# Retention rounds with three unread 512-column products each, normalisations on ScalarE, and output tiles begun before the last mixed rows, in a two-layer attention block on Trainium2

## The chip, the core and the metric

The kernel runs on one core of one Trainium2 chip and uses the core's engines together: TensorE (PE in the profile; PEld is its loading of weights), VectorE (DVE), ScalarE (ACT), GpSimd (POOL), and SyncE (SP), which issues the DMAs. The metric is the time in microseconds of one launch, which covers both layers. An engine runs its instructions in the order in which they are written; between engines the order is made by semaphores alone.

## The reference

Two layers, each of a token mixer and a feed-forward part, on 1024 tokens of width 1024, in float32. The mixer has three kinds of heads whose results stand side by side: differential attention (512 columns), MLA (256) and retention (256). What the change touches is retention, the third:

```python
rel = pos[:, None] - pos[None, :]
decay = where(rel >= 0, exp(max(rel, 0) * log_gamma[h]), 0)
xi   = exp((pos + 1) * log_gamma)       # per head
zeta = exp((c - 1 - pos) * log_gamma)
inner = einsum('bnihd,bnjhd->bnhij', q, k) * decay
inner = einsum('bnhij,bnjhe->bnihe', inner, v)
new_state = einsum('bjhd,bjhe->bhde', k * zeta, v) + exp(c * log_gamma) * state
cross = einsum('bnihd,nbhde->bnihe', q, prev_states) * xi
o = inner + cross                       # (o - mean) * rsqrt(var + 1e-6), per head of 64
return silu(g) * (o * gn_w + gn_b)
```

There are 4 heads of 64 columns, in chunks of c = 128 tokens. The mixed rows then go through an output projection, `x = x + mixed @ w_out` (1024 by 1024), and through the feed-forward part.

## The kernel before

Every product of the reference is done as three products of TensorE on operands that are split in a high and a low part (hi·hi, hi·lo, lo·hi, the helper `split` with `products`, L718). ScalarE makes a high part by a copy that rounds, and VectorE or GpSimd the low part by subtracting it. An operand that has to stand with its columns on the partitions is transposed by TensorE into a PSUM bank (`take_ring` hands out the banks in turn and waits until an old one has been read), and the two evictions of the bank, ScalarE's high part and VectorE's low part, free it.

A layer runs through these stages, on each engine in the same order: norm and transposes of x, differential attention, MLA, retention, transposes of the mixed rows, output projection, feed-forward part. The projections for retention (q, k, v and gate of a unit in one row `r_z[n]` of 512 columns) are made during the MLA steps, by `ret_project`, in the bank Z_BANK (4), and VectorE turns q and k there by their rotary angles (`ret_rotate`).

**The retention rounds** are the stage that the change rewrites. A unit is one pair of heads in one chunk of 128 tokens: 16 units, 8 chunks of each of 2 pairs. TensorE's loop (L1034 to L1040) does in one round the transposes of one unit, the inner and state products of the unit before it and the output products of the one before that:

- `ret_transpose` (L978): three transposes 128x128, of q, k and of q times xi. ScalarE has made q times xi and k times zeta in `r_xzt` by four scalings of 64 columns per unit (`ret_scaled`). ScalarE and VectorE evict the three as `rt_hi` and `rt_lo` (128x384, L1820).
- `ret_inner` (L991): k·q for the two heads, three products each; then, except in the last chunk of a pair, the state product of k times zeta (`rk_hi`, `rk_lo`) with v (`rv`, high and low part side by side). VectorE multiplies the inner result by the decay table (`r_at`, L1830), and multiplies the state by its chunk decay and adds the product (`r_st`, L1840). ScalarE makes the high parts of both and GpSimd the low ones.
- `ret_output` (L1010): per head two products with `r_at` and, but for a pair's first chunk, two with the state (L1027, L1028).
- VectorE sums the two halves (`r_sum`, L1849), takes the moments (L1853, L1858), and once GpSimd has made the inverse root it normalises each of the two heads (`r_norm`, L1867). GpSimd multiplies by gn_w, adds gn_b and multiplies by the gate into `mixed_rows` (`ret_finish`).

The same rounds carry the split of the first half of w_out: four parts, ScalarE's high (L1158) and GpSimd's low (L2147), in rounds 0 to 3. SP loads decay, gn_w and gn_b (counted together by one semaphore, `ret_in`) when the last attention output has been read, since they lie where attention's buffers were, and the first use of any of them, `r_at` of unit 0, waits for all three.

**After the rounds** TensorE transposes all 8 tiles of `mixed_rows`: 64 transposes in 16 blocks of four (`transpose_rows`, L749), each block evicted to `ht_hi` by ScalarE (L1170) and to `ht_lo` by VectorE (L1607), over a ring of four banks. They start when all units are finished for the first half of the tiles. Then come 16 output tiles of 128 tokens by 512 columns, q = 0 to 15 in bank q % 4, each of 24 products 128x512 (8 blocks k of rows, three products each). VectorE adds a tile to X; from q = 4 on TensorE waits for the addition of tile q - 4. X comes back from DRAM in two halves (`x_back0`, `x_back1`), as its place holds other things in between; SP asks for the first when the transposes of the first four tiles are through, and for the second when all are.

Of the kernel before, what the change touches and what calls it, by code (L numbers as in the profile page):

```python
# [8 lines left out]
F32 = mybir.dt.float32  # L9
F32R = mybir.dt.float32r  # L10
# [92 lines left out]
def mla_back_rings():  # L103
# [25 lines left out]
    r_vlo=2 * T, r_take=2 * T, r_xz=2 * T, r_kzhi=2 * T, r_kzlo=2 * T, ri_done=2 * T, r_at=2 * T, r_athi=2 * T, r_atlo=2 * T,  # L129
    ro_done=2 * T, rs_done=2 * (T - 1), r_st=2 * (T - 1), r_sthi=2 * (T - 1), r_stlo=2 * (T - 1),  # L130
    r_bn=2 * T, r_mv=2 * T, r_ms=2 * T, r_rstd=2 * T, r_on=2 * T, r_gw=2 * T, r_gb=2 * T, r_mx=2 * T,
# [43 lines left out]
def constants():  # L175
# [6 lines left out]
    xi = np.exp((pos[:, None] + 1.0) * log_gamma[None, :])  # L182
    zeta = np.exp((P - 1.0 - pos)[:, None] * log_gamma[None, :]) * RET_DIM ** -0.5
    for p in range(RET_PAIRS):
        c[:, C_XZ + 4 * p:C_XZ + 4 * p + 2] = xi[:, 2 * p:2 * p + 2]
        c[:, C_XZ + 4 * p + 2:C_XZ + 4 * p + 4] = zeta[:, 2 * p:2 * p + 2]
        c[:64, C_CD + p] = np.exp(P * log_gamma[2 * p])
        c[64:, C_CD + p] = np.exp(P * log_gamma[2 * p + 1])
# [7 lines left out]
    rel = pos[None, :] - pos[:, None]  # L196
    decay = np.where(rel[:, None, :] >= 0, np.exp(np.maximum(rel, 0.0)[:, None, :] * log_gamma[None, :, None]), 0.0)
    return c, (decay * RET_DIM ** -0.5).astype(np.float32).reshape(P, RET_HEADS * P)


def hybrid_block_kernel(nc, x, positions, attn_norm, w_in, diff_lam_q1, diff_lam_k1, diff_lam_q2, diff_lam_k2,
                        diff_subln, mla_q_norm, mla_w_uq, mla_kv_norm, mla_w_ukv, ret_gn_w, ret_gn_b, w_out,
                        ffn_norm, w_gate, w_up, w_down, final_norm, out):
    const_np, decay_np = constants()
    const_dram = nc.inline_tensor(const_np, name="const_table").ap()
    decay_dram = nc.inline_tensor(decay_np, name="decay_table").ap()
# [79 lines left out]
    decay = sb("decay", [P, RET_PAIRS, 2 * P], F32, EREG)  # L286
    gn_w = sb("gn_w", [P, RET_W], F32, EREG + 2 * KB)
    gn_b = sb("gn_b", [P, RET_W], F32, EREG + 3 * KB)
    rt_hi = [sb(f"rt_hi{i}", [P, 3, P], F32R, HT + 12 * KB + 1536 * i) for i in range(3)]
    rt_lo = [sb(f"rt_lo{i}", [P, 3, P], F32R, HT + 17 * KB + 1536 * i) for i in range(3)]  # L290
# [3 lines left out]
    rv = [sb(f"rv{i}", [P, 2, 2, RET_DIM], F32R, HT + (22 + i) * KB) for i in range(5)]  # L294
# [8 lines left out]
    r_xzt = [sb(f"r_xzt{i}", [P, 4, 64], F32, HT + (35 + i) * KB) for i in range(3)]  # L303
    r_at = sb("r_at", [P, 2 * P], F32, HT + 38 * KB)
    r_at_hi = [sb(f"r_at_hi{i}", [P, 2 * P], F32R, HT + (8 + i) * KB) for i in range(2)]
    r_at_lo = [sb(f"r_at_lo{i}", [P, 2 * P], F32R, HT + (10 + i) * KB) for i in range(2)]
    r_st = sb("r_st", [P, P], F32, MREG + 13 * KB)
    r_sum = [sb(f"r_sum{i}", [P, 2, RET_DIM], F32, MREG + 13 * KB + 512 + 512 * i) for i in range(2)]
# [2075 lines left out]
```

## Time and profile before

| | us |
|---|---|
| median of 3 runs | 2777.3 |
| the runs | 2774.96, 2777.3, 2779.53 |
| the profiled execution: its time | 2776.76 |
| its span in the trace | 2775.0 |
| TensorE busy | 2597.4 (94%) |
| VectorE busy | 1560.8 (56%) |
| ScalarE busy | 1107.1 (40%) |
| GpSimd busy | 1039.7 (37%) |

The busy shares are means over the whole span. TensorE counts as busy for as long as a product or transpose of it is under way, at either of its clocks; the clock that it was granted stands in a row of its own of the page, and in a column of the table by stage (1.00 is 2.4 GHz, 0.50 is 1.2 GHz). In a timeline the time of a product reaches into the next one's, so the distance of two starts tells what one costs. The first layer's retention rounds lie at 561 to 636 us and the second's at 1933 to 2007.

### The profile page before, as it was taken

How to read it: one execution, taken by the hardware profiler on the slowest of the kernel's cores; microseconds unless marked ns; L12 is line 12 of the kernel's file. 1: busy time of each engine (PE TensorE's matmuls, PEld its weight loads, DVE VectorE, ACT ScalarE, POOL GpSimd, SP SyncE). 2: the span in 40 equal slices, each digit the busy share in tenths (PEclk: the TensorE clock that was granted, in tenths of full speed). 3: DMA queues.
4: the chain of work that ended last, by engine and by line, in shares of the span. 5: the costliest groups of instructions: out<-in, count | busy, mean ns of one | idle time of the engine just before them, and what ended most of it. 6: DMA issues, size and time to landing. Idle time of an engine off the chain costs nothing. (4 is left out here: it accounts for less than half of the span.)

```text
span 2775.0 us, 43012 instructions
## 1 busy us (share of the span) xinstructions
PE 2597.4 (94%) x12940; PEld 2228.0 (80%) x12940; DVE 1560.8 (56%) x3033; ACT 1107.1 (40%) x2567; POOL 1039.7 (37%) x1229
## 2 busy tenths in 40 slices
PE   6999988889999999999989998988998999999997
PEld 5999877767778888888879998776776888888886
DVE  4666554473455445477656765544726544545785
ACT  4444543352532232244444455434515232322444
POOL 3455522183154544301034554222812555442012
PEclk9999999958999999999999999998599999999999
DMA  5111101121223332483331101012022323335633
GB/s 173 28 36 41 30 15 37 38 84 61 103 73 110 106 110 93 148 292 96 103 107 31 34 19 39 6 37 89 32 91 76 111 84 104 110 104 207 231 95 122
DMA packets 238651, 243.06 MB, mean 88 GB/s; under 512 B 27904, under 2 KB 170752, under 8 KB 238464
## 3 DMA queue, kind: packets, MB, share of 16 engines
q1 hardware_dynamic: 238464, 240.83, 27.0%
q8 instruction: 86, 1.41, 0.2%
q14 instruction: 101, 0.83, 0.1%
HBM read 173.14 MB, written 67.63 MB: 87 GB/s over the span
## 5 line engine op out<-in xcount | busy, mean ns | idle before, releaser
L2319 POOL TENSOR_TENSOR fw_a_lo<-fw_a_raw,fw_a_hi 128x512 fp32r<-128x512 f32 x132 | 178.7, 1354 | 520.6 <-DVE fw_s_raw L1913 520.6
L2319 POOL TENSOR_TENSOR fw_s_lo<-fw_s_raw,fw_s_hi 128x512 fp32r<-128x512 f32 x176 | 231.4, 1327 | 54.6 <-ACT fw_s_hi L1422 54.6
L718 PE MATMUL banks<-ht_hi,da_hi 128*128 128x512 f32 x496 | 192.9, 389 | 0.0
L718 PE MATMUL banks<-ht_lo,da_hi 128*128 128x512 f32 x496 | 192.9, 389 | 0.0
L718 PE MATMUL banks<-ht_hi,da_lo 128*128 128x512 f32 x496 | 192.9, 389 | 0.0
L718 PE MATMUL banks<-w_diff_hi,ht_hi 128*128 128x384 f32 x512 | 181.2, 354 | 6.3 <-DVE ht_lo L1609 4.3
L718 PE MATMUL banks<-w_diff_hi,ht_lo 128*128 128x384 f32 x512 | 172.9, 338 | 0.0
L718 PE MATMUL banks<-w_diff_lo,ht_hi 128*128 128x384 f32 x512 | 172.8, 337 | 0.0
L2158 POOL TENSOR_TENSOR qk_rot<-rope_a,rope_b 128x512 f32<-128x512 f32 x64 | 82.6, 1291 | 211.7 <-DVE rope_b L1638 211.7
L1666 DVE TENSOR_REDUCE stats<-banks 128x1 f32<-128x1024 f32 (+3 forms) x192 | 138.3, 747 | 29.8 <-PE banks L919 24.9
L718 PE MATMUL banks<-h_t_hi,fw_s_hi 128*128 128x512 f32 x352 | 139.9, 398 | 12.2 <-DVE h_t_lo L1917 8.2
L718 PE MATMUL banks<-h_t_lo,fw_s_hi 128*128 128x512 f32 x352 | 139.0, 395 | 0.0
L718 PE MATMUL banks<-h_t_hi,fw_s_lo 128*128 128x512 f32 x352 | 138.9, 395 | 0.0
L1496 ACT ACTIVATE u_two<-u_two 128x512 f32<-128x512 f32 x42 | 26.6, 633 | 281.1 <-DVE u_two L2024 281.1
L718 PE MATMUL banks<-ht_hi,fw_a_hi 128*128 128x512 f32 x352 | 137.4, 390 | 0.9 <-POOL fw_a_lo L2319 0.9
L718 PE MATMUL banks<-ht_hi,fw_s_hi 128*128 128x512 f32 x352 | 137.0, 389 | 0.0
L718 PE MATMUL banks<-ht_hi,fw_a_lo 128*128 128x512 f32 x352 | 137.0, 389 | 0.0
L718 PE MATMUL banks<-ht_lo,fw_s_hi 128*128 128x512 f32 x352 | 137.0, 389 | 0.0
L718 PE MATMUL banks<-ht_lo,fw_a_hi 128*128 128x512 f32 x352 | 137.0, 389 | 0.0
L718 PE MATMUL banks<-ht_hi,fw_s_lo 128*128 128x512 f32 x352 | 137.0, 389 | 0.0
L1981 DVE TENSOR_TENSOR da_lo<-da_raw,da_hi 128x512 fp32r<-128x512 f32 x154 | 117.1, 760 | 22.6 <-ACT da_hi L1473 22.6
L1233 ACT ACTIVATE pt_hi<-banks 128x512 fp32r<-128x512 f32 (+1 forms) x96 | 43.7, 490 | 208.2 <-PE banks L821 208.2
(351 smaller groups left out, 7647.5 us busy)
## 6 DMA issues: line engine op xcount, KB each, us to landing
da_raw<-act_scratch SPq DMA_DIRECT2D x154, 256.0 KB, 2.7
fw_a_raw<-in_w_gate_dram SPq DMA_DIRECT2D x88, 256.0 KB, 3.0
act_scratch<-act_s SPq DMA_DIRECT2D x66, 256.0 KB, 3.0
w_diff_raw<-in_w_in_dram SPq DMA_DIRECT2D x24, 512.0 KB, 6.0
fw_a<-in_w_up_dram SPq DMA_DIRECT2D x44, 256.0 KB, 3.2
fw_a_raw<-in_w_up_dram SPq DMA_DIRECT2D x44, 256.0 KB, 2.9
act_scratch<-act_zero SPq DMA_DIRECT2D x44, 256.0 KB, 2.4
act_scratch<-act_one SPq DMA_DIRECT2D x44, 256.0 KB, 2.8
```

Source lines behind the costliest of these rows:

```text
L718: mm = pe.matmul(bank, lhsT, rhs, start=first and i == 0, stop=last and i == len(pairs) - 1, skip_group_check=resumes)
L1233: act.activation(hi[:, b:b + n, :], banks[:, TR_BANKS[r % 2], 0:n * P].rearrange("p (b n) -> p b n", n=P), ACT.Copy).then_inc(S["tr_hi"], 1)
L1496: act.activation(u2[1 - m][:], u2[1 - m][:], ACT.Silu).then_inc(S["u_g1"], 1)
L1666: dve.tensor_reduce(neg_max[:, a % 2, m:m + 1], SCORE[j % 2][:, 0:(t + 1) * P], AX_X, ALU.max, negate=True)\
L1981: dve.tensor_tensor(a[1][:], a[2][:], a[0][:].bitcast(F32), ALU.subtract)
L2158: return pool.tensor_tensor(dst[:] if copies > 1 else dst[:].unsqueeze(2), a, b, ALU.add)
L2319: pool.tensor_tensor(w[1][:], w[2][:], w[0][:].bitcast(F32), ALU.subtract).then_inc(S["f_lo"], 1)
```

## The change

**Retention.** The scalings by xi and zeta go. With age = (pos + 1)·log_gamma, v is multiplied by exp(-age)·64^-0.5 (in place in `r_z`, one VectorE multiplication of 128x128 per unit, in `ret_rotate` during the MLA stage). Then the inner result needs only a causal mask of ones and zeros, one for all heads (`causal`, 64 KB in place of 256 KB), the state needs its chunk decay once more where it is split, and the result is the old one divided by exp(age) in each row, which the normalisation takes out again; for that its epsilon is multiplied by exp(-2·age). A unit has two transposes in place of three, `rt_hi` and `rt_lo` are 128x256, `r_xzt` and `ret_scaled` are gone. The low part of the state moves from GpSimd to VectorE (`ret_state_low`). The normalisation moves from VectorE to ScalarE (`ret_normed`), with an offset that VectorE makes for two units at a time (`ret_offset`); GpSimd makes the roots and applies gain and bias for two units at a time, and the units are finished later (a round is now numbered u, and unit n is normalised on ScalarE in round n + 7).

**Unread products.** `keep_clock(n)` issues n products of the identity with the identity repeated four times, 128x512, into Z_BANK, which nothing reads then: 1 and 2 in each of the last five MLA steps, 3 ahead of the wait for `o_free`, 3 behind the transposes of rounds 0 to 2, and in every round 1 behind the inner and state products and 2 behind the output products.

**Behind the rounds.** The transposes of mixed rows no longer wait for retention where they don't need it: the blocks k = 0 to 5 (768 columns of the other heads) of both halves are transposed at once, and ScalarE and VectorE evict two such blocks in each round from u = 18 (`mixed_blocks`), among the last normalisations. The output tiles q = 0 to 3 are done in two pieces: 18 products each on k = 0 to 5, then the 16 transposes of k = 6 and 7, and then the other 6 products each. SP asks for the two halves of X when the transposes of k = 6 and 7 are half through and through, and for the second half of w_out after retention's unit 9.

```diff
-    arrives(decay[:], decay_dram.rearrange("p (a n) -> p a n", a=RET_PAIRS), "ret_in")
+    arrives(causal[:], causal_dram, "ret_in")
...
-    sp.wait_ge(S["r_xz"], L * PER["r_xz"] + T + 2)
-    sp.wait_ge(S["r_vlo"], L * PER["r_vlo"] + T + 2)
+    sp.wait_ge(S["r_mx"], L * PER["r_mx"] + T // 2 + 1)
...
-        sp.wait_ge(S["tr_done"], L * PER["tr_done"] + RING - NORM2_RINGS - 2 * KD + (half + 1) * KD)
+        sp.wait_ge(S["tr_done"], L * PER["tr_done"] + RING - NORM2_RINGS - 2 + 2 * half)
...
+    def keep_clock(n):
+        for _ in range(n):
+            pe.matmul(banks[:, Z_BANK, :].rearrange("p (b n) -> p b n", b=4), ident_r[:],
+                      ident_r[:].unsqueeze(1).to_broadcast([P, 4, P]), start=True, stop=True)
...
     for a in MLA_STEPS:
+        if a >= MLA_UNITS - 2:
+            keep_clock(1)
         ret_project(a, 0)
         mla_probs(a - 1)
+        if a >= MLA_UNITS - 2:
+            keep_clock(2)
...
+    keep_clock(3)
     pe.wait_ge(S["o_free"], L * PER["o_free"] + PER["o_free"])
-    for n in range(1, RET_UNITS + 3):
...
+    for u in RET_STEPS:
+        if u < RET_UNITS:
+            ret_transpose(u // T, u % T)
+            keep_clock(0 if u > 2 else 3)
+        if 0 <= u - 1 < RET_UNITS:
+            ret_inner((u - 1) // T, (u - 1) % T)
+            keep_clock(1)
+        if 0 <= u - 2 < RET_UNITS:
+            ret_output((u - 2) // T, (u - 2) % T)
+            keep_clock(2)
...
-    transpose_rows(mixed_rows[:, 0:4, :], "r_mx", T + 4)
-    transpose_rows(mixed_rows[:, 4:8, :], "r_mx", 2 * T)
+    for half in range(2):
+        transpose_rows(mixed_rows[:, 4 * half:4 * half + 4, :], "mix_in", 16, range(KD - 2))
...
+    for t in range(4):
+        products(banks[:, t, :], out_pairs(0, t, range(KD - 2)))
+    for half in range(2):
+        pe.wait_ge(S["r_mx"], L * PER["r_mx"] + T // 2 + 2 * half + 2)
+        transpose_rows(mixed_rows[:, 4 * half:4 * half + 4, :], "mix_in", 16, range(KD - 2, KD))
     ring_empty()
...
+def ret_normed(n):
+    m, i = n // 2, n % 2
...
+    for j in range(2):
+        st = act.activation(r_norm[b][:, i, 64 * j:64 * j + 64], r_sum[m % 3][:, i, j, :], ACT.Identity,
+                            bias=r_nb[:, b, 2 * i + j:2 * i + j + 1], scale=r_rs[:, b, 2 * i + j:2 * i + j + 1])
...
+    for u in RET_STEPS:
+        if 0 <= u - 3 < RET_UNITS:
+            ret_take(u - 3)
+        if u < RET_UNITS:
+            ret_low(u)
+        if 0 <= u - 1 < RET_UNITS:
+            ret_inner(u - 1)
+        if 0 <= u - 3 < RET_UNITS:
+            ret_moments(u - 3)
+        if u >= 6 and u % 2 == 0 and u // 2 - 3 < RET_UNITS // 2:
+            ret_offset(u // 2 - 3)
+        if u + 2 < RET_UNITS:
+            ret_low_v(u + 2)
+        if 0 <= u - 1 < RET_UNITS:
+            ret_state_low(u - 1)
+        for half, k in mixed_blocks(u):
+            low_rows(half, None, [k])
```

TensorE's order in a steady round, from the state product to the end of the round, before (`rv` and `rk` are v and k of the unit, `r_at` the decayed inner result, `r_st` the split state):

```order
L718 MATMUL banks<-rv_191,rk_hi_183 128x128 x2
L718 MATMUL banks<-rv_191,rk_lo_185 128x128
L1027 MATMUL banks<-rv_190,r_at_hi_215 128x128
L1028 MATMUL banks<-rv_190,r_at_lo_217 128x64
L1027 MATMUL banks<-r_st_223,rt_hi_177 128x128
L1028 MATMUL banks<-r_st_223,rt_lo_180 128x64
L1027 MATMUL banks<-rv_190,r_at_hi_215 128x128
L1028 MATMUL banks<-rv_190,r_at_lo_217 128x64
L1027 MATMUL banks<-r_st_223,rt_hi_177 128x128
L1028 MATMUL banks<-r_st_223,rt_lo_180 128x64
L980 REGISTER_ALU
L982 MATMUL banks<-ident,r_z_198 128x128
```

And with the change:

```order
L722 MATMUL banks<-rv_187,rk_hi_184 128x128 x2
L722 MATMUL banks<-rv_187,rk_lo_186 128x128
L971 MATMUL banks<-ident_r 128x512
L1041 MATMUL banks<-rv_191,r_at_hi_211 128x128
L1042 MATMUL banks<-rv_191,r_at_lo_213 128x64
L1041 MATMUL banks<-r_st_219,rt_hi_178 128x128
L1042 MATMUL banks<-r_st_219,rt_lo_181 128x64
L1041 MATMUL banks<-rv_191,r_at_hi_211 128x128
L1042 MATMUL banks<-rv_191,r_at_lo_213 128x64
L1041 MATMUL banks<-r_st_219,rt_hi_178 128x128
L1042 MATMUL banks<-r_st_219,rt_lo_181 128x64
L971 MATMUL banks<-ident_r 128x512 x2
```

One wide product now stands between the state product and the output products, two behind these; the transposes of the next round follow the pair.

In the diff the last loop is VectorE's, the one with `ret_normed` ScalarE's.

VectorE's order in a round before, from the eviction of the transposes (`rt_lo`) to the next round:

```order
L1820 TENSOR_TENSOR rt_lo_180<-banks,rt_hi_177 128x384
L1827 REGISTER_ALU
L1830 TENSOR_TENSOR r_at<-banks,decay 128x256
L1833 REGISTER_ALU
L1840 SCALAR_TENSOR_TENSOR r_st<-r_st,stats,banks 128x128
L1867 TENSOR_SCALAR r_norm_231<-r_sum_220,stats 128x64 x2
L1811 TENSOR_TENSOR rv_190<-r_z_200,rv_190 128x2x64
L1849 TENSOR_REDUCE r_sum_219<-banks 128x128
L1853 BN_STATS stats<-r_sum_219 128x6 x2
L1858 BN_AGGR stats<-stats 128x2 x2
L1591 REGISTER_ALU
```

And with the change:

```order
L1852 TENSOR_TENSOR rt_lo_180<-banks,rt_hi_177 128x256
L1859 REGISTER_ALU
L1862 TENSOR_TENSOR r_at<-banks,causal 128x256
L1865 REGISTER_ALU
L1872 SCALAR_TENSOR_TENSOR r_st<-r_st,stats,banks 128x128
L1887 BN_STATS stats<-r_sum_217 128x6 x2
L1892 BN_AGGR stats<-stats 128x2 x2
L1908 SCALAR_TENSOR_TENSOR stats<-stats 128x4
L1843 TENSOR_TENSOR rv_190<-r_z_200,rv_190 128x2x64
L1900 SCALAR_TENSOR_TENSOR r_st_221<-r_st,stats,r_st_221 128x128
L1880 TENSOR_REDUCE r_sum_218<-banks 128x128
```

The two normalisations (`r_norm`) are gone from VectorE; the offset of two units (`stats` 128x4, in every second round) and the low part of the state (L1900) are new, and the sum `r_sum` is now ahead of the eviction of the next round.

TensorE's order from the last output products to the transposes of the mixed rows, before:

```order
L1028 MATMUL banks<-r_st_222,rt_lo_180 128x64
L1043 REGISTER_ALU
L749 MATMUL banks<-ident,mixed_rows 128x128 x16
L739 REGISTER_ALU
L749 MATMUL banks<-ident,mixed_rows 128x128 x4
L739 REGISTER_ALU
L749 MATMUL banks<-ident,mixed_rows 128x128 x4
```

With the change the transposes start in the same place, for k = 0 to 5:

```order
L1042 MATMUL banks<-r_st_220,rt_lo_180 128x64
L971 MATMUL banks<-ident_r 128x512 x2
L753 MATMUL banks<-ident,mixed_rows 128x128 x16
L743 REGISTER_ALU
L753 MATMUL banks<-ident,mixed_rows 128x128 x4
```

and the last four blocks stand behind the 72 products of the first pieces:

```order
L722 MATMUL banks<-w_o_lo,ht_hi 128x512
L722 MATMUL banks<-w_o_hi,ht_lo 128x512
L743 REGISTER_ALU
L753 MATMUL banks<-ident,mixed_rows 128x128 x4
L743 REGISTER_ALU
L753 MATMUL banks<-ident,mixed_rows 128x128 x4
L743 REGISTER_ALU
L753 MATMUL banks<-ident,mixed_rows 128x128 x4
L743 REGISTER_ALU
L753 MATMUL banks<-ident,mixed_rows 128x128 x4
L736 REGISTER_ALU
L722 MATMUL banks<-w_o_hi,ht_hi 128x512
```

So four blocks of transposes, of k = 6 and 7, and the wait for their evictions (the register instruction of L736), have moved into the output projection.

## Rows read from the trace of the kernel before

**Rows 1.** The page's slices: the clock granted to TensorE, in tenths.

```profile
PEclk9999999958999999999999999998599999999999
```

**Rows 2.** Busy us by stage: PE, PEld, DVE, ACT, POOL; clock, DMA share, GB/s.

```profile
548.00:550.00 2.00, 0.47 (x2) 0.24 (x2) 0.41 (x2) 1.99 (x10) 0.29 (x1) 1.00 0.16 35
...
555.30:561.00 5.70, 0.12 (x1) 0.00 (x0) 0.00 (x0) 0.00 (x0) 0.00 (x0) 0.50 0.91 203
```

**Rows 3.** The same table: rounds, transposes, first output tiles.

```profile
561.00:636.00 75.00, 66.74 (x291) 56.23 (x292) 57.31 (x163) 43.73 (x144) 65.74 (x121) 0.50 0.17 62
...
606.00:626.00 20.00, 20.00 (x92) 16.72 (x91) 16.82 (x52) 11.45 (x43) 18.23 (x39) 0.50 0.30 107
635.50:638.80 3.30, 3.30 (x17) 3.21 (x16) 1.48 (x8) 1.70 (x3) 2.31 (x5) 0.50 0.00 0
...
648.70:652.40 3.70, 3.68 (x9) 2.92 (x10) 0.00 (x0) 0.00 (x0) 1.16 (x1) 0.55 1.01 319
652.40:660.00 7.60, 7.60 (x35) 6.21 (x34) 0.69 (x1) 0.00 (x0) 0.00 (x0) 1.00 0.36 143
```

**Rows 4.** TensorE timeline of one late round: start us, us, engine, line, operation.

```profile
1991.23 0.47 PE L982 MATMUL banks<-ident,r_z 128*128 128x128 f32 x1
...
1992.07 0.48 PE L718 MATMUL banks<-rt_hi 64*128 64x128 f32 x2
...
1992.91 0.69 PE L718 MATMUL banks<-rv,rk_hi 128*128 128x128 f32 x2
...
1993.61 0.41 PE L1027 MATMUL banks<-rv,r_at_hi 128*128 128x128 f32 x1
1993.82 0.36 PE L1028 MATMUL banks<-rv,r_at_lo 128*128 128x64 f32 x1
1994.11 0.47 PE L1027 MATMUL banks<-r_st,rt_hi 64*128 64x128 f32 x1
...
1994.67 0.47 PE L1027 MATMUL banks<-rv,r_at_hi 128*128 128x128 f32 x1
...
1995.80 0.47 PE L982 MATMUL banks<-ident,r_z 128*128 128x128 f32 x1
```

**Rows 5.** VectorE timeline of one round of the first layer.

```profile
615.79 0.41 DVE L1849 TENSOR_REDUCE r_sum<-banks 128x128 f32<-128x256 f32 x1
...
616.91 0.53 DVE L1820 TENSOR_TENSOR rt_lo<-banks,rt_hi 128x384 fp32r<-128x384 f32 x1
...
617.79 0.35 DVE L1840 SCALAR_TENSOR_TENSOR r_st<-r_st,stats,banks 128x128 f32<-128x128 f32 x1
618.38 1.12 DVE L1867 TENSOR_SCALAR r_norm<-r_sum,stats 128x64 f32<-128x64 f32 x2 [0.25 <-POOL stats L2116]
...
619.94 0.41 DVE L1849 TENSOR_REDUCE r_sum<-banks 128x128 f32<-128x256 f32 x1
```

**Rows 6.** Waits, us in total, times, longest; DMA, us to landing.

```profile
DVE r_at L1830 <- DMA gn_b<-in_ret_gn_b_dram: 6.6, 1, 6.6
...
decay<-decay_table SPq DMA_DIRECT2D x1, 256.0 KB, 2.6
```

**Rows 7.** TensorE timeline, last transposes and first output products.

```profile
635.44 3.59 PE L749 MATMUL banks<-ident,mixed_rows 128*128 128x128 f32 x16
...
648.72 0.53 PE L718 MATMUL banks<-w_o_hi,ht_hi 128*128 128x512 f32 x1 [1.90 <-DVE ht_lo L1607]
...
649.90 0.63 PE L718 MATMUL banks<-w_o_hi,ht_hi 128*128 128x512 f32 x1
...
652.46 0.40 PE L718 MATMUL banks<-w_o_hi,ht_hi 128*128 128x512 f32 x1
...
663.17 0.39 PE L718 MATMUL banks<-w_o_hi,ht_lo 128*128 128x512 f32 x1
```

**Rows 8.** ScalarE timeline of the evictions; DMA issues of X.

```profile
640.28 7.17 ACT L1170 ACTIVATE ht_hi<-banks 128x512 fp32r<-128x512 f32 x12 [0.62 <-PE banks L749]
...
X<-x_scratch SPq DMA_DIRECT2D x2, 2048.0 KB, 9.3
```

More of the change, by code:

```diff
@@ L383, in hybrid_block_kernel @@
     sin_m = keep("sin_m", [P, T, 2, 16])
[L384 removed]
+    stats = keep("stats", [P, 208])
     taken = [0]
@@ L481, in hybrid_block_kernel, with mixed_blocks @@
         ROUND_RET = (0, 17)
+        RET_STEPS = range(RET_UNITS + 8)
+        ROUND_OUT = {0: 0, 2: 1, 4: 2, 6: 3}
+        MIXED_BLOCKS = [(half, k) for half in range(2) for k in range(KD - 2)]
+        def mixed_blocks(u):
+            return MIXED_BLOCKS[2 * (u - RET_UNITS - 2):2 * (u - RET_UNITS - 1)] if u >= RET_UNITS + 2 else []
         FINAL_POOL = 4
@@ new lines, in _ @@
+                for t in range(4):
[3 more added lines that the diff above has]
+                    transpose_rows(mixed_rows[:, 4 * half:4 * half + 4, :], "mix_in", 16, range(KD - 2, KD))
+                ring_empty()
+                for q in range(2 * T):
+                    c, t = q // T, q % T
+                    if q < 4:
+                        products(banks[:, q, :], out_pairs(c, t, range(KD - 2, KD)), first=False, resumes=True).then_inc(S["out_done"], 1)
+                    else:
+                        if q == T:
+                            pe.wait_ge(S["w_hi"], L * PER["w_hi"] + PARTS * (CH_OUT + 2))
+                            pe.wait_ge(S["w_lo"], L * PER["w_lo"] + CH_OUT + 2)
+                        pe.wait_ge(S["out_add"], L * PER["out_add"] + q - 3)
+                        products(banks[:, q % 4, :], out_pairs(c, t, range(KD))).then_inc(S["out_done"], 1)
+                    if q >= 4:
@@ L1920, in _ @@
                 for half in range(2):
-                    low_rows(half, None)
+                    low_rows(half, None, range(KD - 2, KD))
                 for q in range(2 * T):
@@ L2301, in _ @@
[L2301 to L2311 removed]
+                    pool.tensor_tensor(r_norm[b][:], r_norm[b][:], w, ALU.mult).then_inc(S["r_gw"], 1)
@@ new lines, in ret_finish @@
+                    st.then_inc(S["r_mx"], 1)
+                for u in RET_STEPS:
+                    if u < RET_UNITS:
+                        ret_low_k(u)
+                    if 0 <= u - 1 < RET_UNITS:
+                        ret_inner(u - 1)
+                    if u >= 5 and u % 2 == 1 and (u - 5) // 2 < RET_UNITS // 2:
+                        ret_root((u - 5) // 2)
+                    if u >= 9 and u % 2 == 1:
+                        ret_finish((u - 9) // 2)
+                    if u in ROUND_OUT:
+                        weights(CH_OUT, [ROUND_OUT[u]])
```

260 lines of the change are left out of this document (113 added, 147 removed).

## Prediction

> **What bounds the kernel now.** I read the page's slices first [rows 1]: the clock line dips in the ninth slice and again in the 29th, once per layer. The table by stage places it [rows 2, 3]. TensorE still has 1.00 at 548 to 550, where it is busy for 0.47 us of 2, and the lower of its two levels (0.50 granted, 1.2 GHz) from 555, where it waits until 561; then come 75 us of retention at 0.50, and as much in the second layer. Inside, the stretch 606 to 626 has TensorE busy for 20.00 us of 20 at 0.50, with DVE at 16.82 and POOL at 18.23: three engines are nearly full, and whichever gets longer sets the round. The timeline of one late round [rows 4] gives TensorE 4.57 us from transposes to transposes (1991.23 to 1995.80): 0.84 to the inner products, 0.84 for them, 0.70 for the state product, 2.19 for the output products. The DVE of a round that it sets itself [rows 5] repeats after 4.15 us (615.79 to 619.94), of which the two normalisations take 1.12. The wait at the start belongs to neither: DVE's first r_at waits 6.6 us for gn_b [rows 6], and TensorE's second inner product waits for r_at.
>
> **The change part by part**, for one layer, on the times of the first.
>
> The tables. The DVE waits for the same three transfers, of which decay (256 KB, landed after 2.6 us) becomes 64 KB [rows 6]. 192 KB at the stretch's 203 GB/s [rows 2] is 0.9 us, the bounds are 0 and 0.9; I take **-0.7**, since gn_b, the last of them, is untouched. Idle TensorE remains from about 555 to 561, so the clock falls as before: no wide product is issued in it, as they stand ahead of or behind the waiting inner product. Those in the last attention steps and the first three rounds (15, 3 and 9) fill idle time [rows 2].
>
> TensorE's round. One transpose of three goes (0.21 like other narrow products, 1993.61 to 1993.82 [rows 4]), three products of 512 columns come. Their price isn't in the trace before; the nearest row is the output projection at 0.50, where such products start 0.43 us apart (six from 649.90 to 652.46 [rows 7]). Bounds: 0, if they fill gaps between weight loads, and 0.43 + 0.21 each, if a load is exposed as well. I take 0.43, as the load of the next weights hides under a wide product in those rows. If the clock stays at 0.50 the round is 4.57 - 0.21 + 1.27 = **5.63 us**, and TensorE alone sets it.
>
> DVE's round loses the normalisations (1.12) and a third of the eviction of rt (0.53, by the row of 256 columns, 0.41: 0.12), and gains the low part of the state (like the other 128x128 operations, 0.35) and half an offset (0.05): 4.15 - 1.24 + 0.40 = 3.3 us. POOL loses the state's low part and does gains, biases and roots for two units at once: below DVE. ACT drops four scalings and takes two normalisations: below too. With the clock at 0.50 all of this lies beside TensorE and **is worth nothing**; only at 1.00 would it count.
>
> From TensorE's second inner product to the end of the last output product, before: 561.96 to 635.5, 73.5 us (early rounds of up to 5.7 us with the w_o work, then 4.15 to 4.57). After, starting at 561.25: the rest of round 2 (0.84 + 0.70 + 0.43 + 0.85, and output products without their cross terms, 2.19 - 2 x 0.56) 3.9; 13 rounds of 5.63, less 0.70 where unit 7 has no state product and 1.12 where unit 8 has no cross term, 71.4; inner 15 and output 14 with their wide products 4.3; output 15 2.2. Together 81.8, ending at 643.0: **+7.5 us**, the 0.7 included.
>
> The end of the stage. Before: from 635.44 to the first projection at 648.72, 13.3 us (64 transposes, evictions, 1.90 of waiting), then 384 products 0.2275 apart (47 from 652.46 to 663.17) and nine of them at half clock (+1.8) [rows 7]: 102.4. Now: two wide products 0.85; twelve blocks of four transposes, evicted by ACT at 0.60 each [rows 8] between five rounds of normalisations at about 0.55, of which the last may start after the eighth eviction, as there are four banks: 8 x 0.60 + 5 x 0.55 + 0.75 for its transposes, 8.3; 72 products of the first pieces 16.4 (the last mixed rows are ready by then); four more blocks with their evictions exposed, 4 x 0.60 + the 1.90 that TensorE waited before its first product [rows 7], 4.3; 312 products 71.0; and a wait for X, whose first 2 MB are asked for about 1.0 into these blocks, take 9.3 [rows 8] and then want an addition of 0.69 [rows 3] before the fifth tile, while the blocks and four tiles fill 4.3 + 5.5: 1.2. Sum 102.0: **-0.4**. The transposes hidden behind normalisations come back as the second round of evictions and as the late X. Bounds -3 and +2.
> That first product after the transposes runs at 1.00 or 0.50 by what the transposes do to the clock; in [rows 3] it rose from 0.50 to 1.00 over 3.3 us in which TensorE did transposes alone.
> The Trainium skill (TensorE: Matmul & The Clock Gate, Part 4) says that transposes do not count as work for the clock; by that the sum would be 1.8 us a layer higher. The trace speaks against it.
>
> The attention stage. DVE gets one more multiplication (128x128, about 0.3) per retention unit, behind the projections of that stage, where TensorE is the full engine; with the wide products ahead of the last attention outputs I put **+0.3** (bounds 0 and 1.5).
>
> Sum: 7.5 - 0.4 + 0.3 = 7.4 us a layer, 14.8 for two, on the profiled execution of 2776.8 us (span 2775.0): 2791.6. The median of the runs shown is 2777.3, within 0.5 of it.
>
> **The rivals.** The question is the clock, and no row of before has this mixture, so I compare what TensorE did in stretches with either level. It rose after 3.3 us of transposes back to back and during wide products back to back (0.55 in the mean of 648.7 to 652.4, then 1.00) [rows 3]; it stayed at 0.50 through rounds in which TensorE counts as always busy, because of narrow products spaced by weight loads. In a round of 5.63 us the wide products take 1.27 and the transposes 0.4; between the first wide one and the pair lie 2.19 us of narrow output products, and behind the pair again inner and state products for 1.54. That is far nearer to a round of before than to back-to-back work. I therefore expect 0.50.
>
> Rival 1, **the clock is held** (the other side): once the wait is over the mixture brings the clock back at once. Then TensorE's round is about half of 5.63, 2.8, DVE's 3.3 binds, with the waits between engines 3.45. One layer: 3.9 + 13 x 3.45 + 3.3 = 52.1 instead of 73.5, with the 0.7, the 0.4 and the 0.3 -22.2 us, two layers -44: 2732. It decides from the point where the clock is once at 1.00 in these rounds: the same wide products then come every 3.45 us instead of every 5.63, so a level once reached will probably last. For it: at 548 to 550 the clock was still 1.00 with TensorE busy 0.47 of 2 us [rows 2], so it does not fall at a short lull. Against: it must first rise at 1.2 GHz.
> The Trainium skill (same page, Part 1) says that sustained activity releases the throttle and idleness brings it back; read as the busy time of TensorE, it would give this rival's 2732. The 20.00 us of 20 at 0.50 [rows 3] speak against that reading, and I give it no more than the chance below.
>
> Rival 2, **it comes back late**, or in some rounds, as rounds and clock shift against each other: half of the rounds at either level, -8 us a layer, 2761.
>
> Rival 3, **the wide products are free**: they fill gaps between narrow products, the round stays near 4.36 to 4.6 us and TensorE's 73.5 us are repeated; with the 0.7, 0.4 and 0.3 it is 2775, no change. Against it: TensorE's starts in [rows 4] are 0.21 to 0.36 apart throughout, with no gap of 0.43.
>
> **How the numbers follow.** Forecast 0.52; rival 1 0.22, rival 2 0.18, rival 3 0.08. 0.2% (5.5 us) is about what a measurement of this kernel can tell from no change. The predicted time is that of the forecast, 2791.6; alone its range is 2779 to 2802 (the product's price, the end's bounds). Forecast, rivals 2 and 3 hold 0.78, a little of it above the top, so the range has to take in rival 1 as well: 2728 to 2802. Slower: the forecast less a tenth of it at its lower end, 0.47. Same: that tenth and most of rival 3, 0.10. Faster: rivals 1 and 2 and the rest, 0.43.
>
> **What would show it.** Right: a clock line at 0.50 from 557 to past 640, TensorE's rounds 5.6 us with DVE and POOL near 60% busy; last output product near 643 in the first layer; r_at's wait a little shorter; four blocks of transposes after 72 wide w_o products, and an idle TensorE of 2 to 4 us behind them; DVE's first X addition waiting for the X transfer. Wrong: a granted clock of 1.00 in the rounds (then 3.4 to 3.6 us a round, ended by DVE), no wait for gn_b left, or first pieces waiting for w_o or for the banks.

## The result and the profile after

The changed kernel takes 2794.1 us (median of 16 runs, 2778.0 to 2800.6), the kernel before 2774.8 on the same chips (16 runs, 2770.4 to 2783.9): a ratio of 1.0065, 95% interval 1.0051 to 1.0079, about 18 us slower. The profiled execution took 2794.3 with a span of 2792.4, 17.4 more than before. 2791.6 was forecast, with 2779 to 2802 for the likeliest case and 2728 to 2802 with the rivals.

The page's line of the granted clock, one digit for a fortieth of the span, shows the two dips where they were [rows 1]:

```profile
PEclk9999999958999999999989999998599999999999
```

The table by stage (the same columns as in [rows 3]) shows, in this order: the wait, in which the clock falls; the rounds, forty and twenty microseconds with a full TensorE at 0.50; the transposes at 1.00; and the second block of transposes at 668, behind which the clock falls once more (in this layer; in the second it does not):

```profile
556.00:558.00 2.00, 0.00 (x0) 0.00 (x0) 0.00 (x0) 0.00 (x0) 0.40 (x1) 0.80 0.89 146
566.00:606.00 40.00, 40.00 (x154) 32.34 (x155) 18.21 (x74) 16.26 (x51) 18.97 (x27) 0.50 0.01 2
606.00:626.00 20.00, 20.00 (x80) 15.94 (x80) 9.16 (x35) 8.56 (x29) 10.99 (x19) 0.50 0.01 1
646.00:650.00 4.00, 3.20 (x24) 2.37 (x23) 3.43 (x7) 4.00 (x11) 3.07 (x7) 1.00 0.79 299
668.00:672.00 4.00, 2.10 (x19) 1.77 (x17) 2.48 (x4) 3.24 (x6) 0.16 (x1) 1.00 0.38 83
672.00:676.00 4.00, 4.00 (x12) 3.22 (x13) 0.00 (x0) 2.60 (x3) 4.00 (x2) 0.66 1.00 404
```

In [rows 3] VectorE was busy 16.82 of 20 us and GpSimd 18.23; now 9.16 and 10.99. TensorE alone sets the round. Its timeline of one round:

```profile
611.25 1.22 PE L971 MATMUL banks<-ident_r 128*128 128x512 f32 x2
612.27 0.41 PE L998 MATMUL banks<-ident,r_z 128*128 128x128 f32 x1
...
614.36 0.73 PE L971 MATMUL banks<-ident_r 128*128 128x512 f32 x1
614.90 0.31 PE L1041 MATMUL banks<-rv,r_at_hi 128*128 128x128 f32 x1
...
616.99 1.22 PE L971 MATMUL banks<-ident_r 128*128 128x512 f32 x2
618.00 0.41 PE L998 MATMUL banks<-ident,r_z 128*128 128x128 f32 x1
```

A round takes 5.74 us (611.25 to 616.99, and 612.27 to 618.00), against 4.57 in [rows 4]. The unread product behind the state product costs 0.54 to the next start, the pair 1.02 (616.99 to 618.00).

The waits at the start of the stage (us in total, times, longest), answering to [rows 6]:

```profile
DVE r_at L1862 <- DMA gn_b<-in_ret_gn_b_dram: 4.1, 1, 4.1
PE banks L722 <- DVE r_at L1862: 3.6, 1, 3.6
```

gn_b was waited for 4.1 us instead of 6.6. The end of the stage in the first layer, TensorE's timeline, answering to [rows 7]:

```profile
641.96 1.22 PE L971 MATMUL banks<-ident_r 128*128 128x512 f32 x2
642.98 4.25 PE L753 MATMUL banks<-ident,mixed_rows 128*128 128x128 f32 x24
...
668.12 1.91 PE L753 MATMUL banks<-ident,mixed_rows 128*128 128x128 f32 x16
671.93 0.50 PE L722 MATMUL banks<-w_o_hi,ht_hi 128*128 128x512 f32 x1 [1.90 <-DVE ht_lo L1637]
...
673.52 0.63 PE L722 MATMUL banks<-w_o_hi,ht_hi 128*128 128x512 f32 x1
```

The second group of four blocks is 16 transposes in 1.91 us; then 1.90 of waiting for the eviction, six products at the higher clock, and from 673.52 the lower one for some 3 us. VectorE's first addition to X waited for the transfer, as forecast. In the first layer, where the lower clock made the tiles ahead of it longer, TensorE had no wait from it. In the second the clock stayed at 1.00 behind the second transposes, and TensorE waited 1.55 us for it:

```profile
678.05 2.48 DVE L1973 TENSOR_TENSOR X<-X,banks 128x512 f32<-128x512 f32 x4 [6.18 <-DMA X<-x_scratch]
...
2061.12 0.50 PE L722 MATMUL banks<-w_o_hi,ht_hi 128*128 128x512 f32 x1 [1.55 <-DVE X L1973]
```

Where the time went, by the starts of the same instructions in both traces (us, each figure rounded by itself):

| | before | after | change |
|---|---|---|---|
| layer 1: last attention transpose | 550.5 | 550.3 | -0.2 |
| from there to the first `r_at` | 11.0 | 8.0 | -2.9 |
| from there to the end of the last output product | 73.9 | 83.6 | +9.7 |
| from there to the last w_out product | 105.8 | 106.1 | +0.3 |
| feed-forward part, and layer 2 up to its last attention transpose | 1183.0 | 1183.6 | +0.6 |
| layer 2: to the first `r_at` | 8.8 | 8.5 | -0.3 |
| to the end of the last output product | 73.7 | 83.6 | +9.9 |
| to the last w_out product | 105.9 | 106.4 | +0.5 |
| all | | | +17.5 |

### The profile page after: what moved, and what is told of

The parts are those of the page before. It is cut to its first block and busy times, and to the rows that moved or that the text cites. A ratio compares the mean times of both kernels' runs of the same rounds, so it can differ in the third digit from the quotient of the medians.

```text
span 2792.4 us, 43064 instructions
## 1 busy us (share of the span) xinstructions
PE 2636.9 (94%) x13058; PEld 2255.2 (81%) x13058; DVE 1532.8 (55%) x3045; ACT 1095.8 (39%) x2503; POOL 1009.5 (36%) x1137
```

## The experiments

Eleven kernels. All times are medians, and each ratio is to runs of the kernel before made beside it on the same chip, whose median was 2774.8 to 2777.4; the changed kernel's 2794.1 stands beside 2774.8. A "wide" product is one of 512 columns, a "narrow" one of 64 or 128; "three a round" means the three unread wide products of a steady round. The letters A, B and C name the theories of the expectations.

### What the unread products cost

**No unread products.**

```diff
 def keep_clock(n):
-    for _ in range(n):
+    for _ in range(0 * n):
```

> The changed kernel without any unread product (47 in the rounds of a layer and 27 ahead of them). Theory A (each of those in the rounds costs TensorE about 0.5 us at the lower clock and buys nothing, the rest of the change is a gain): TensorE's round 5.74 - 1.55 + 0.1 = 4.3 us at a granted clock of 0.50, the stage about 21 us shorter per layer, 2751. Rival B (they fill time in which TensorE would wait for the others anyway): about 2790. Rival C (they do hold the clock ahead of the rounds or in some of them): no better than the changed kernel, 2790 to 2800, with TensorE waiting longer at the start.

(By the loop there are 48 in the rounds of a layer, not 47; the trace of the changed kernel has 75 a layer in all.)

Measured: 2754.2 us (2752.5 to 2755.3), ratio to before 0.9929 (0.9916 to 0.9942). Two starts of a round's first transpose, of TensorE's timeline:

```profile
598.55 0.47 PE L998 MATMUL banks<-ident,r_z 128*128 128x128 f32 x1
...
602.91 0.47 PE L998 MATMUL banks<-ident,r_z 128*128 128x128 f32 x1
```

The round is 4.36 us, which is 4.57 less the one transpose (0.21), at 0.50. So three unread products cost 5.735 - 4.36 = 1.375 us, 0.46 each, and theory A holds: 40 us of the changed kernel are paid for nothing, and the rest of the change gains 21 against the kernel before. B and C fall, though a part of C is true: without the unread products ahead of the rounds the clock is lost sooner in the first layer (0.50 from 550.5 us instead of 557.2), which the wait for gn_b makes worthless. Where the rest gains is not where I looked. The steady rounds are little shorter than before. In the kernel before five successive rounds began at 564.4, 571.0, 576.6, 583.1 and 589.5, so 6.3 us a round with the split of w_out on GpSimd among them (GpSimd busy for 18.50 us of the 20 from 580 to 600); here four rounds take 17.4 us instead of 25.1. The relief of GpSimd and VectorE pays in those.

**The kernel before with the three unread products alone.** The definition of `keep_clock`, and a wait of TensorE for Z_BANK ahead of the rounds, go in with them; what counts is:

```diff
     ret_inner((n - 2) // T, (n - 2) % T)
+    keep_clock(1)
 if n >= 3:
     ret_output((n - 3) // T, (n - 3) % T)
+    keep_clock(2)
```

> The kernel before with the three unread products a round alone. TensorE's rounds of 4.57 us become 5.95 (1.375 for the three, from the changed kernel's 5.735 against 4.36 without them); the first five rounds, which GpSimd sets at 5.6 to 6.5, hardly change: about +15 us a layer, 2807. Rival (the clock comes up in GpSimd's rounds or later): 4.15 us rounds set by VectorE, 2765 or less.

Measured: 2799.9 us (2798.3 to 2801.2), ratio 1.0084 (1.0070 to 1.0098). Two starts of a round:

```profile
627.72 0.42 PE L983 MATMUL banks<-ident,r_z 128*128 128x128 f32 x1
...
633.66 0.42 PE L983 MATMUL banks<-ident,r_z 128*128 128x128 f32 x1
```

5.94 us a round, as expected, at 0.50. In total it is 7 us less than forecast. The early rounds of this run begin 7.2, 6.5, 5.9 and 5.9 us apart, and TensorE waited for r_at at the start only 2.6 us in the first layer (6.7 in the kernel before) and 4.4 in the second (4.6); how the rest of the 7 us comes about is open. Without the change's algebra the unread products do the same harm.

### Whether the mixture holds the clock, and what loses it

**The wait filled.** 19 more unread products ahead of the second inner product, where TensorE otherwise waits for gn_b:

```diff
-    keep_clock(0 if u > 2 else 3)
+    keep_clock(0 if u > 2 else 3 + 19 * (u == 2))
```

> The changed kernel with 19 more unread products in the wait for gn_b (ahead of the second inner product), about 4.4 us at the higher clock. Theory A1 (the mixture of the rounds would hold the clock, but cannot raise it again after the wait): granted clock 1.00 through the rounds, rounds of about 3.45 us, ended by VectorE, 30 us less per layer, 2734. Rival A2 (three wide products in a round are too few at either level): the clock falls within the first rounds, rounds of 5.74 again, 2790 to 2800.

Measured: 2755.2 us (2751.8 to 2768.6), ratio 0.9938 (0.9919 to 0.9957): between what the two theories gave. The table by stage of this run tells why:

```profile
562.00:590.00 28.00, 28.00 (x188) 22.82 (x187) 22.12 (x82) 19.32 (x63) 21.30 (x27) 1.00 0.26 102
594.00:626.00 32.00, 32.00 (x122) 25.69 (x123) 14.72 (x60) 12.02 (x37) 20.19 (x34) 0.51 0.00 1
```

Up to 590 the clock is at 1.00 in a full TensorE, 28 us and some eight rounds; behind 594 the same mixture runs at 0.51 to the end. In between, TensorE's timeline (two starts of a round, then the products around the wait), and GpSimd's (gn_w, mixed_rows, the low parts of k and of r_at):

```profile
585.26 0.27 PE L998 MATMUL banks<-ident,r_z 128*128 128x128 f32 x1
...
588.54 0.27 PE L998 MATMUL banks<-ident,r_z 128*128 128x128 f32 x1
...
591.23 0.34 PE L722 MATMUL banks<-rt_hi 64*128 64x128 f32 x2
...
592.94 0.43 PE L722 MATMUL banks<-rv,rk_hi 128*128 128x128 f32 x2 [1.15 <-issue]
```

```profile
589.73 0.74 POOL L2338 TENSOR_TENSOR r_norm<-r_norm,gn_w 128x256 f32<-128x256 f32 x1
...
591.42 0.92 POOL L2345 TENSOR_TENSOR mixed_rows<-r_norm,r_z 128x128 f32<-128x128 f32 x2
592.30 0.45 POOL L2313 TENSOR_TENSOR rk_lo<-r_z,rk_hi 128x128 fp32r<-128x128 f32 x1
592.72 0.72 POOL L2318 TENSOR_TENSOR r_at_lo<-r_at,r_at_hi 128x256 fp32r<-128x256 f32 x1
```

At 1.00 a round is 3.28 us (585.26 to 588.54). Round 10 (588.54 to 590.92, counted by u) is short, since unit 8 has no cross products, and in and behind it GpSimd has the gains of a pair of units to finish (589.73 to 592.3) before it can make the low part of k of unit 10. The profile names no releaser of TensorE's 1.15 us (`issue`), but the kernel has it wait there for that low part, which ends at 592.75. The clock falls within the next 2 us; in the second layer the same wait (1.15 us) ended at 1955.4, and the clock fell there too. So in both layers the mixture held the clock up to this short wait, and at 0.50 it did not come back by itself in 32 us.

**The mask alone.** The first `r_at` waits for the mask by a semaphore of its own, not for gn_w and gn_b:

```diff
-    arrives(causal[:], causal_dram, "ret_in")
+    arrives(causal[:], causal_dram, "causal_in")
...
-    dve.wait_ge(S["ret_in"], L * PER["ret_in"] + PER["ret_in"])
+    dve.wait_ge(S["causal_in"], L * PER["causal_in"] + PER["causal_in"])
```

> The changed kernel, but the first r_at waits for the mask alone (a semaphore of its own), not for gn_w and gn_b. The mask lands 1.9 us after its issue, gn_b 3.9 us. If the clock falls all the same: the wait of 3.6 us before the second inner product shortens by about 2 us a layer and nothing else changes, 2790. If the shorter wait lets the clock stay up and the rounds hold it: 2730. If both happen in different executions: anything between, with a wide spread.

Measured: 2762.6 us in 11 runs that spread from 2749.0 to 2768.8, ratio 0.9942 (0.9924 to 0.9960). The third case, in one execution. First layer:

```profile
554.00:558.00 4.00, 3.92 (x13) 3.09 (x14) 1.34 (x4) 1.85 (x6) 1.15 (x3) 0.57 0.21 51
562.00:586.00 24.00, 24.00 (x160) 19.40 (x158) 19.61 (x75) 16.62 (x52) 18.98 (x25) 1.00 0.29 114
594.00:622.00 28.00, 28.00 (x108) 22.63 (x109) 13.23 (x51) 11.19 (x35) 17.30 (x30) 0.50 0.00 1
```

and second layer:

```profile
1926.00:1998.00 72.00, 72.00 (x275) 57.80 (x274) 32.56 (x135) 28.41 (x89) 38.64 (x60) 0.50 0.01 3
```

In the first the clock fell at 554 and came back by itself at 558, in the first rounds, which have three, four and six unread products and few narrow ones; it held for more than 30 us and was lost at 591.8, behind a wait of 1.16 us. In the second, where waits of 0.47, 0.26 and 0.20 us stood within 5 us, it fell at about 1923 and stayed at 0.50 for 72 us of a full TensorE. The same three products a round, at either level, for tens of microseconds.

**Six a round.**

```diff
-    keep_clock(1)
+    keep_clock(2)
...
-    keep_clock(2)
+    keep_clock(4)
```

> The changed kernel with twice the unread products in a round (2 behind inner and state, 4 behind output). If the mixture still stays at 0.50: a round of 5.74 + 1.5 = 7.3 us, 22 us more per layer, 2838. If six are enough to raise the clock after the wait: rounds of 3.5 to 3.8 us at 1.00 for all but the first few, 2745 to 2755.

Measured: six runs at 2744.7, 2754.2, 2765.6, 2787.0, 2788.3 and 2792.6. The profiled one:

```profile
566.00:618.00 52.00, 52.00 (x324) 42.28 (x323) 34.09 (x136) 28.22 (x93) 37.48 (x58) 1.00 0.01 3
1918.00:1970.00 52.00, 52.00 (x189) 41.85 (x189) 20.73 (x81) 17.88 (x57) 22.19 (x29) 0.50 0.06 22
1974.00:1990.00 16.00, 16.00 (x102) 13.12 (x101) 10.97 (x42) 8.97 (x30) 12.38 (x22) 1.00 0.01 2
```

First layer: clock back after the wait, then 52 us at 1.00. Second layer: 52 us at 0.50 (a full TensorE, 1918 to 1970), with rounds of 7.02 us, then back at 1.00 in steady rounds. Six can raise the clock, but not at once or surely. So even twice the unread products do not replace a clock that was never lost, and a round at 1.00 costs 3.98 us with them (starts at 572.0, 576.0, 580.0), against 3.28 with three.

**Both waits filled.** The 19 of before, and 5 more ahead of the inner products of round 10. These do not stand in the second wait; they stretch the round ahead of it (3.54 us instead of 2.38), so that GpSimd is done in time:

```diff
-    keep_clock(0 if u > 2 else 3)
+    keep_clock({0: 3, 1: 3, 2: 22, 10: 5}.get(u, 0))
```

> The run that filled the first wait lost the clock again at 592.9 and 1956, behind a wait of 1.15 us for GpSimd in the short round without cross products. This one fills both: 19 more unread products in the wait for gn_b and 5 more ahead of the inner products of round 10. Theory A1 (three wide products a round hold the clock, a wait loses it, and they cannot raise it again): granted clock 1.00 to the end of the stage, seven rounds more at 3.3 instead of 5.7 us, 12 us less per layer than with the first wait filled, 2730. Rival A2 (the clock falls by itself after some tens of us at this mixture): falls again near 590, 2755 to 2760.

Measured: 2735.3 us (2733.6 to 2747.6), ratio 0.9863 (0.9842 to 0.9883).

```profile
562.00:606.00 44.00, 43.59 (x290) 35.26 (x291) 34.09 (x133) 29.96 (x97) 36.68 (x54) 1.00 0.08 33
```

44 us at 1.00, through the place where it had been lost: A2, which had it fall near 590, is wrong. One rival is not excluded: five wide products in a row may have renewed the clock, apart from the wait that they took away. Part of the 5 us missing against 2730 is that the clock falls at the end of the rounds after all. In the first layer there is one more wait, of TensorE for GpSimd's low part ahead of the last output products (us in total, times, longest), and the clock falls 1.6 us behind it for some 3 us:

```profile
PE banks L1041 <- POOL r_at_lo L2318: 1.7, 1, 1.7
```

In the second layer it falls at 1956.75, for 10 us, and there TensorE had not waited longer than 0.18 us since the rounds began:

```profile
1954.00:1958.00 4.00, 4.00 (x23) 3.21 (x23) 2.94 (x12) 2.28 (x7) 3.28 (x6) 0.84 0.00 0
1958.00:1962.00 4.00, 4.00 (x14) 3.04 (x13) 1.33 (x8) 1.59 (x5) 3.70 (x8) 0.50 0.00 0
```

This is in round 16, the first without transposes and without a state product: 14 narrow products and the three wide ones. So A1 holds for the steady rounds, but a wait is not the only thing behind which the clock falls.

**The first wait removed instead of filled.**

```diff
-    keep_clock(3)
+    keep_clock(8)
     pe.wait_ge(S["o_free"], L * PER["o_free"] + PER["o_free"])
...
-    keep_clock(0 if u > 2 else 3)
+    keep_clock({0: 3, 1: 3, 2: 6, 10: 5}.get(u, 0))
```

together with the mask's own semaphore.

> As the run before, but the first wait is removed and not filled: the first r_at waits for the mask alone, and 8 unread products stand before the wait for o_free, 6 in round 2, 5 more in round 10. If waits are what loses the clock: 1.00 throughout, and the stage begins about 2 us earlier per layer than with the wait filled: 2726. If the clock is lost in the first rounds in some executions: 2730 to 2775, with a wide spread.

Measured: 2734.5 us (2731.3 to 2736.1), ratio 0.9845 (0.9831 to 0.9858); no wide spread.

```profile
562.00:606.00 44.00, 43.66 (x288) 35.25 (x288) 34.17 (x135) 30.31 (x98) 36.15 (x53) 1.00 0.16 64
610.00:618.00 8.00, 7.16 (x29) 6.64 (x30) 2.67 (x9) 3.96 (x10) 7.11 (x13) 0.50 0.26 84
```

1.00 through the steady rounds, 0.50 at the end of them. The wait that is left there does not explain it: the pair of unread products ahead of it already takes 0.96 us, where a pair takes 0.73 at 1.00, and the records of the clock have its fall at 608.76, while the wait begins at 609.38:

```profile
608.42 0.96 PE L971 MATMUL banks<-ident_r 128*128 128x512 f32 x2
610.84 0.45 PE L1041 MATMUL banks<-rv,r_at_hi 128*128 128x128 f32 x1 [1.46 <-POOL r_at_lo L2318]
```

In the second layer it falls at 1960.44, again in round 16 and with no wait over 0.16 us ahead of it in the steady rounds. The earlier start that I had counted on did not come: the first `r_at` is at 558.7 and 1911.3 us, in the run with the wait filled at 558.4 and 1910.0. What the first wait cost was the clock, not its length.

**The same without the three a round**, from round 3 on:

```diff
-    keep_clock(1)
+    keep_clock(1 if u <= 2 else 0)
...
-    keep_clock(2)
+    keep_clock(2 if u <= 2 else 0)
```

> The run with mask alone and filled waits, without the three unread products in a round from round 3 on (those ahead of the rounds, in rounds 0 to 2 and the 5 in round 10 stay). Theory A1 (the three per round are what holds the clock): it falls within the first rounds, rounds of 4.36 us as in the run without any, 2750. Rival A3 (filling the waits is enough, the narrow products alone hold the clock at the higher level): rounds of 3.3 us at 1.00, 2732.

Measured: 2747.8 us (2747.0 to 2754.7), ratio 0.9906 (0.9891 to 0.9921).

```profile
564.00:568.00 4.00, 4.00 (x18) 3.29 (x19) 2.97 (x11) 2.63 (x7) 2.85 (x3) 0.50 0.35 132
568.00:606.00 38.00, 37.38 (x171) 30.84 (x170) 22.97 (x93) 20.68 (x68) 25.51 (x40) 0.54 0.00 1
...
590.00:594.00 4.00, 3.38 (x27) 2.91 (x26) 2.69 (x12) 2.36 (x8) 1.85 (x4) 0.85 0.01 2
```

The clock falls in the second round that has only narrow products, at 564 (behind a wait of 0.44 us), and at 1919 in the second layer, in the first such round (behind one of 0.19 us), and most rounds are at 4.36 us again: A3 falls. Up to there it had been kept, so without the three a round it is not held. The 0.85 at 590 to 594 belongs to the five unread products of round 10: in the first layer they brought the clock back, from 591.2 to 594.6, and the narrow rounds behind them lost it again. In the second layer they did not.

**The same with two a round.**

```diff
-    keep_clock(2)
+    keep_clock(2 if u <= 2 else 1)
```

> The same with two unread products a round, one behind inner and state and one behind output. If two are enough: 3.3 us a round at 1.00, 2734. If they are not: rounds of 4.36 + 0.92 = 5.3 us at 0.50, 2780. If it depends on how the rounds fall: between, with a wide spread.

Measured: 2768.1 us (2765.7 to 2774.1, 11 runs), ratio 0.9980 (0.9969 to 0.9991).

```profile
562.00:580.00 18.00, 17.72 (x92) 14.34 (x92) 13.08 (x47) 10.41 (x29) 12.53 (x16) 0.72 0.32 126
580.00:600.00 20.00, 20.00 (x77) 15.74 (x77) 8.11 (x32) 8.27 (x29) 10.97 (x16) 0.50 0.00 1
...
1970.00:1974.00 4.00, 4.00 (x29) 3.23 (x29) 3.46 (x15) 3.06 (x10) 1.53 (x3) 1.00 0.01 2
```

Lost at about 570 in this layer and 1939 in the other, with no wait just ahead of it but one of 0.17 to 0.18 us; the run with three a round had one of 0.16 and kept the clock. Rounds of 5.3 us follow (starts at 575.75, 581.06, 586.37). In the second layer the five unread products of round 10 brought it back, at 1969.6, and it held for some three rounds, to 1979.8. Two a round did not hold it in this kernel, three did through the steady rounds.

### The end of the stage, and the best kernel

**Undivided output tiles**, in the kernel without unread products:

```diff
-    pe.wait_ge(S["tr_free"], L * PER["tr_free"] + first_half)
-    for t in range(4):
-        products(banks[:, t, :], out_pairs(0, t, range(KD - 2)))
...
-        products(banks[:, q, :], out_pairs(c, t, range(KD - 2, KD)), first=False, resumes=True).then_inc(S["out_done"], 1)
+        products(banks[:, q, :], out_pairs(c, t, range(KD))).then_inc(S["out_done"], 1)
```

> The kernel without unread products (2754.2), with the first four output tiles undivided: all transposes stand ahead of all products of the output projection, so the last mixed rows are waited for. By the ledger of the traces the two pieces are worth nothing (+0.4 us a layer for the whole end of the stage): within 2 us of 2754. Rival (the pieces hide the last normalisations): TensorE waits some 4 us a layer for the last mixed rows, 2762.

Measured: 2751.8 us (2748.9 to 2756.6), against 2754.2 with the pieces: no loss, perhaps 2 us gained; the two ranges overlap, so which is better stays open. The wait that the pieces were to cover is 0.24 us:

```profile
632.78 1.09 PE L753 MATMUL banks<-ident,mixed_rows 128*128 128x128 f32 x8 [0.24 <-POOL mixed_rows L2342]
```

**All together:** the mask alone, the waits filled, 6 more unread products ahead of the last output products, undivided tiles.

```diff
 if 0 <= u - 2 < RET_UNITS:
+    keep_clock(6 if u == RET_UNITS + 1 else 0)
     ret_output((u - 2) // T, (u - 2) % T)
     keep_clock(2)
```

> The run with mask alone and filled waits (2734.5), with 6 more unread products ahead of the last output products, where TensorE waited 1.5 us for GpSimd and the clock fell for some 10 us, and with the first output tiles undivided (2 us in the run without unread products). If the clock is kept through that wait: the last output products 1.5 us and the transposes behind them 2 to 3 us sooner per layer, with the undivided tiles 2726. If not: 2733.

Measured: 2727.4 us (2723.2 to 2733.7), ratio 0.9823 (0.9808 to 0.9838): 47 us faster than the kernel before, 67 faster than the changed one.

```profile
PEclk9999999999999999999999999999999999999999
```

The page's clock line has no dip left, but the clock was not kept through round 16: it is at 0.50 from 609.4 to 612.8 and, in the second layer, from 1957.7 to 1964.5. The wait for GpSimd is gone there, so the fall does not need it. Of the 7 us gained against 2734.5 the share of each part is not known.

## Why the prediction was right

**The clock** was the question, and the forecast, 0.50 through all the rounds in both layers, is what the profile shows. Its reason, that the mixture of a round is nearer to narrow work than to back-to-back wide products, is at most half of the truth, and no run varied the narrow work to test it. It fits the clock's not coming back (72 us at 0.50 with the mask alone); it does not say that the same mixture holds a clock that is up, which it did for 44 us on end. Rival 1 had this right ("a level once reached will probably last"), and its 3.45 us a round came out at 3.28. Its "against", that the clock must first rise at 1.2 GHz, decided. Rival 2, the clock back late or in part, happens too: two of 16 runs of the changed kernel took 2778 us and the other 14 2791 or more, with a mean clock of 0.956 and 0.959 over the span instead of about 0.951. In which rounds it came back there is not known, as they have no profile.

**The number** is nearer than the change. +14.8 us was forecast; the two traces differ by 17.4, the medians by 19.3. The time comes within 2.5 us because the profiled execution that it was added to (2776.8) lay 2 us above the median of the 16 runs (2774.8). The stated range, 2728 to 2802, reaches down to rival 1, so a time inside it says little; the granted clock and the length of a round are what bears the forecast out.

**TensorE's round**: 5.63 forecast, 5.74 measured. The wide product was put at 0.43 and cost 0.46, and the lost transpose gave 0.21 as taken. Rival 3, free products, is refuted by both kernels that had them added or removed.

**The stage** from the second inner product to the last output product: 81.8 forecast, 83.0 measured (558.93 to 641.96), for which the 0.1 a round is enough (13 rounds). The same stage before was read as starting at 561.96; the trace has 562.09, which changes nothing of weight.

**The tables**: -0.7 forecast, -3.2 measured for the first `r_at` in the first layer (of which 0.2 came before it); from the last attention transpose -2.9 there and -0.3 in the second. The bound of 0.9 was wrong: it took the 192 KB less at the stretch's rate, but gn_b, issued 0.35 us sooner, landed 3.9 us after its issue instead of 6.7. The 3 MB of mixed rows are asked for right behind it in both kernels; that gn_b shares the engines with them for less long is likely and was not tested. In the first layer this made up for the dearer rounds: -2.9 + 9.7 = 6.8, where 7.5 was forecast for both together; that two errors cancel there is luck. In the second layer they did not: -0.3 + 9.9 = 9.6.

**VectorE and GpSimd**: worth nothing at 0.50, as said, against the steady rounds. But I gave the early rounds as up to 5.7 us, and they were up to 6.5, set by GpSimd. In these the relief is worth 8 us a layer, which the unread products then used up. Had I costed the algebra apart from the unread products, I should have found that the change is two changes of opposite sign, -21 and +40 us.

**The end of the stage**: -0.4 forecast, +0.3 and +0.5 measured. The parts: four blocks behind 72 products, 1.91 + 1.90 us (4.3 forecast); in the first layer no wait of TensorE for X (1.2 forecast), but products at half clock behind the second transposes, so that the four tiles took longer; in the second layer the wait, 1.55 us, and no half-clock products. The one replaced the other. The half-clock products behind the first transposes (1.8 us in the kernel before) were gone in both layers. The transposes raised the clock again: 0.50 until about 646, 1.00 from there, with transposes alone from 642.98. The Trainium skill (TensorE: Matmul & The Clock Gate, Part 4) says that transposes do not count for the clock; the runs here disagree.

**Attention**: +0.3 a layer forecast; -0.2, and +0.6 with the feed-forward part, measured.

## What to carry to other kernels

Split a change into its parts before giving it one number: here -21 us and +40 us stood under one name. Work that is added to keep the clock paid here only where the clock was up and no wait cut in. So find the waits first (here a gain vector that the first user did not need, and another engine's batch of work in a short round), and only then add the fill; and where a wait can't be removed, fill that one. Then look at the clock again: here it still fell in the last rounds, where TensorE's work has another mixture. If the clock is down in the profile after such a change, the fill is pure cost, and taking it out is the first thing to try.

## What the runs showed of the hardware

The granted clock of a stretch depended on the level at which it began. The same rounds of 19 narrow and three 512-column products ran at 1.00 for 44 us when they began there and at 0.50 for 72 us when they began at that. Six a round had both levels in one execution and went from 0.50 to 1.00 after 52 us. Five unread products back to back, in round 10, brought a lost clock back in two layers of four. Whether the chip keeps a level for its own sake is not separated from a simpler reading: at 1.00 the rounds are shorter, so the same wide products come every 3.28 us and not every 5.74. Four waits of TensorE of 1.15 to 1.7 us in steady rounds or at their end were each followed by the fall within 2 us. But of eight waits of 1.4 to 1.6 us just ahead of the rounds, among wide products, four were followed by a fall and four were not, and five falls in round 16 (one in the run with both waits filled, two each in the run with the mask alone and fills and in the best kernel) had no wait ahead of them that could explain them. What makes the clock fall there is open. The Trainium skill (TensorE: Matmul & The Clock Gate, Part 1) says that sustained activity releases the throttle and idleness brings it back. The falls behind waits agree with the second half, those in round 16 with TensorE busy do not; 72 us at 0.50 with TensorE counted as busy throughout do not fit the first, if activity is read as the busy time of a profile. Transposes alone, of float32 128x128, were followed by the rise in the changed kernel as in the kernel before, after about 3 us (642.98 to about 646, 635.44 to 638.8).

An unread 512-column product among narrow ones cost 0.46 us at 0.50, hardly more than back to back (0.43 in [rows 7]).
